# Entering the experts tile by tile beside the last products of the layer before

## The reference

```python
def rmsnorm(x, g):
    return x * rsqrt(mean(x * x, -1) + 1e-6) * g

for layer in range(2):
    h = h + mixer(rmsnorm(h, norm_mix_g[layer]))      # ends with a product by w_o
    t = rmsnorm(h, norm_ffn_g[layer])
    grp_logits = t @ w_grp + b_grp                    # 4 groups
    exp_logits = t @ w_exp + b_exp                    # 16 experts
    # best group, its two best experts, softmax weights
    for e in range(16):
        h = h + gate[:, e] * ((silu(t @ w_gate[e]) * (t @ w_up[e])) @ w_down[e])
```

## Time and profile before

| | us |
|---|---|
| median of 3 runs | 1503.54 |
| lowest, highest | 1500.58, 1504.72 |
| the profiled execution | 1504.47 |
| its span | 1502.7 |
| TensorE busy | 1370.2 |
| VectorE busy | 1030.9 |
| ScalarE busy | 854.3 |
| GpSimd busy | 390.1 |

### The profile page before, as it was taken

The page is one execution under the profiler, slowest core; times in us unless marked ns, Lnnn a source line. Parts: engine busy times, 40 slices in busy tenths (PEclk is TensorE's granted clock), DMA queues, the critical chain, the costliest instruction groups (busy, mean ns, idle before and its releaser), DMA issues. The chain is left out here.

```text
span 1502.7 us, 28124 instructions
## 1 busy us (share of the span) xinstructions
PE 1370.2 (91%) x10835; PEld 1071.2 (71%) x10835; DVE 1030.9 (69%) x1374; ACT 854.3 (57%) x1282; POOL 390.1 (26%) x431
## 2 busy tenths in 40 slices
PE   5999897988899889999998699999989899999994
PEld 3476686776774578888876587778777688888872
DVE  5366653556643599999887535775454799998996
ACT  6635551455541368888885425445552488888882
POOL 1022063446550112232323200001120122333312
PEclk9999896989989999999999899999978899999997
DMA  5222300141560689999996341221101899999984
GB/s 176 84 85 84 140 1 15 41 137 58 156 213 0 224 306 390 386 384 382 381 384 230 113 129 57 76 65 57 57 29 62 294 365 386 390 381 377 383 324 174
DMA packets 160579, 299.67 MB, mean 199 GB/s; under 512 B 16974, under 2 KB 32462, under 8 KB 160481
## 3 DMA queue, kind: packets, MB, share of 16 engines
q1 hardware_dynamic: 147968, 269.43, 50.0%
q0 software_dynamic: 11232, 24.61, 4.6%
q10 hardware_dynamic: 1280, 4.26, 0.7%
HBM read 279.96 MB, written 34.60 MB: 209 GB/s over the span
## 5 line engine op out<-in xcount | busy, mean ns | idle before, releaser
L1475 DVE TENSOR_TENSOR moe_wlo<-moe_raw,moe_whi 128x2048 fp32r<-128x2048 f32 x162 | 370.2, 2288 | 43.0 <-ACT moe_whi L1471 38.5
L1471 ACT ACTIVATE moe_whi<-moe_raw 128x2048 fp32r<-128x2048 f32 x192 | 365.3, 1918 | 43.7 <-DMA moe_raw<-in_moe_w_down_dram 19.2
L1482 PE MATMUL all_bank<-moe_whi,moe_xhi 128*128 128x512 f32 x512 | 205.2, 401 | 4.1 <-DVE moe_xlo L1531 4.1
L1483 PE MATMUL all_bank<-moe_wlo,moe_xhi 128*128 128x512 f32 x512 | 200.5, 392 | 0.0
L1484 PE MATMUL all_bank<-moe_whi,moe_xlo 128*128 128x512 f32 x512 | 200.4, 391 | 0.0
L1482 PEld LDWEIGHTS all_bank<-moe_whi,moe_xhi 128*128 128x128 f32 x512 | 96.8, 189 | 26.4 <-DVE moe_xlo L1531 4.4
L1484 PEld LDWEIGHTS all_bank<-moe_whi,moe_xlo 128*128 128x128 f32 x512 | 96.8, 189 | 21.0
L1483 PEld LDWEIGHTS all_bank<-moe_wlo,moe_xhi 128*128 128x128 f32 x512 | 97.1, 190 | 19.0
L1482 PE MATMUL all_bank<-moe_whi,moe_hhi 128*128 128x512 f32 x256 | 100.5, 392 | 4.1 <-issue 2.6
L1484 PE MATMUL all_bank<-moe_whi,moe_hlo 128*128 128x512 f32 x256 | 99.7, 389 | 0.0
L1483 PE MATMUL all_bank<-moe_wlo,moe_hhi 128*128 128x512 f32 x256 | 99.6, 389 | 0.0
(11 more groups left out here) (441 smaller groups left out, 2989.6 us busy)
## 6 DMA issues: line engine op xcount, KB each, us to landing
moe_raw<-in_moe_w_gate_dram SPq DMA_DIRECT2D x64, 1024.0 KB, 12.1
moe_raw<-in_moe_w_up_dram SPq DMA_DIRECT2D x64, 1024.0 KB, 12.5
moe_raw<-in_moe_w_down_dram SPq DMA_DIRECT2D x64, 1024.0 KB, 11.5
attn_xhat<-in_w_kv_dram SPq DMA_DIRECT2D x10, 1024.0 KB, 5.1
out_dram<-all_gain SPq DMA_DIRECT2D x16, 512.0 KB, 5.1
attn_xhat<-in_attn_w_q_dram SPq DMA_DIRECT2D x6, 1024.0 KB, 4.9
all_h<-in_rwkv_w_k_dram SPq DMA_DIRECT2D x4, 1024.0 KB, 9.5
all_h<-in_rwkv_w_v_dram SPq DMA_DIRECT2D x4, 1024.0 KB, 5.0
```

The lines of the kernel that those rows point to most:

```text
L1471: nc.scalar.activation(whi[slot % SPLITS][:, :], raw[slot % 6][:, :], ACT.Copy).then_inc(m["hi_ok"], 1)
L1475: nc.vector.tensor_tensor(wlo[slot % SPLITS][:, :], raw[slot % 6][:, :], whi[slot % SPLITS][:, :].bitcast(fp32), ALU.subtract).then_inc(m[ ...
L1482: nc.tensor.matmul(bank[b][:, :], hi[:, k0 + k, :], wh[:, k, :], start=begin and k == 0, stop=False)
L1483: nc.tensor.matmul(bank[b][:, :], hi[:, k0 + k, :], wl[:, k, :], start=False, stop=False)
```

## The change

Seven things, all in the diff:

1. A set of `front_*` functions does the experts' entry for one tile: squares by half tile with two sums, a shift (mean of the first half's squares plus epsilon) as the bias of the root, reciprocal, norm in two halves, transposes into two banks, copies (first four slices on ScalarE, last four on VectorE), logits of the tile, copy of the rows, sum of the quarters.
2. In `rwkv_chunks` and in `attention` these are placed among the last products, residuals and squares. The whole entry up to the sum of the quarters moves ahead of the meeting of engines, and `moe` starts with the first routing step. TensorE's four leading `keep_busy` matmuls are gone.
3. The normed tokens are stored by SP, one DMA for each tile of 512 KB, instead of one by ScalarE's queue.
4. SP asks for the first four weight pieces (`first_weights`) in the block before: in layer 0 when the last state copy is done, in layer 1 when the last scores are.
5. All 16 blocks of zero rows are written behind the chunks, after the load of `x`, from a part of `raw` that GpSimd clears there; the memset of `gain` in chunk 0 is gone.
6. The router's gain and weights are loaded together in chunk 2.
7. `raw`, the normed tokens and their transposes get one fixed place in SBUF for the whole program (`KEPT`), and the other tiles of each block are arranged around it.

```diff
+FRONT_BANKS = ((4, 5), (6, 7), (4, 5), (0, 1))
+
+
+def front_square(nc, g, f, j, x, junk):
+
+    nc.scalar.activation(junk, g["h"][:, j, 512 * x:512 * x + 512], ACT.Square, accum_out=f[f"part{x}"][:, j:j + 1]).then_inc(f[f"sq{x}"], 1)
+
+
+def front_shift(nc, dve, f, j):
+
+    dve.wait_ge(f["sq0"], j + 1)
+    nc.vector.tensor_scalar(f["shift"][:, j:j + 1], f["part0"][:, j:j + 1], 1.0 / D, NORM_EPS, ALU.mult, ALU.add).then_inc(f["bias"], 1)
+
+
+def front_root(nc, act, f, j):
+
+    act.wait_ge(f["sq1"], j + 1)
+    act.wait_ge(f["bias"], j + 1)
+    nc.scalar.activation(f["rms"][:, j:j + 1], f["part1"][:, j:j + 1], ACT.Sqrt, scale=1.0 / D, bias=f["shift"][:, j:j + 1]).then_inc(f["root"], 1)
+
+
+def front_tile(nc, dve, g, f, layer, j):
+
+    dve.wait_ge(f["root"], j + 1)
+    nc.vector.reciprocal(f["scale"][:, j:j + 1], f["rms"][:, j:j + 1]).then_inc(f["rstd"], 1)
+    if j == 0:
+        dve.wait_ge(g["moe_in"], 80 * (layer + 1))
+    dve.wait_ge(f["rstd"], j + 1)
+    for x in range(2):
+        at = slice(512 * x, 512 * x + 512)
+        nc.vector.scalar_tensor_tensor(out=g["xn"][:, j, at], in0=g["h"][:, j, at], scalar=f["scale"][:, j:j + 1], in1=g["gain"][:, at],
+                                       op0=ALU.mult, op1=ALU.mult).then_inc(f["xn"], 1)
+
+
+def front_store(sp, g, f, io, layer, j):
+
+    sp.wait_ge(f["xn"], 2 * j + 2)
+    sp.dma_start(io[f"xn_dram{layer}"][P * j:P * j + P, :], g["xn"][:, j, :]).then_inc(g["xn_st"], 16)
+
+
+def front_turn(nc, pe, g, f, j):
+
+    if j == 2:
+        pe.wait_ge(f["ev_a"], 1)
+        pe.wait_ge(f["ev_d"], 1)
+    for kt in range(KT):
+        if kt % 4 == 0:
+            pe.wait_ge(f["xn"], 2 * j + kt // 4 + 1)
+        ins = nc.tensor.transpose(g["bank"][FRONT_BANKS[j][kt // 4]][:, P * (kt % 4):P * (kt % 4) + P], g["xn"][:, j, P * kt:P * kt + P], g["ident"][:, :])
+        if kt % 4 == 3:
+            ins.then_inc(f["tr"], 1)
+
+
+def front_pieces(g, j, x):
+
+    return g["xnT"][:, 4 * x:4 * x + 4, P * j:P * j + P], g["bank"][FRONT_BANKS[j][x]][:, :].rearrange("p (k t) -> p k t", k=4)
+
+
+def front_copy_a(nc, act, g, f, j):
+
+    act.wait_ge(f["tr"], 2 * j + 1)
+    dst, src = front_pieces(g, j, 0)
+    nc.scalar.activation(dst, src, ACT.Copy).then_inc(f["ev_a"], 1)
+
+
+def front_copy_d(nc, dve, g, f, j):
+
+    dve.wait_ge(f["tr"], 2 * j + 2)
+    dst, src = front_pieces(g, j, 1)
+    nc.vector.tensor_copy(dst, src).then_inc(f["ev_d"], 1)
+
+
+def front_logits(nc, pe, g, f, layer, j):
+
+    if j == 0:
+        pe.wait_ge(g["moe_in"], 80 * (layer + 1))
+    for kt in range(KT):
+        if kt % 4 == 0:
+            pe.wait_ge(f["ev_d" if kt else "ev_a"], j + 1)
+        c = 32 * (kt % 4)
+        ins = nc.tensor.matmul(g["bank"][2 if j < 3 else 6][c:c + 32, P * j:P * j + P], g["wr"][:, kt, :], g["xnT"][:, kt, P * j:P * j + P], start=kt < 4, stop=kt >= 4)
+    ins.then_inc(f["lg"], 1)
+
+
+def front_rows_a(nc, act, g, f):
+
+    act.wait_ge(f["lg"], 3)
+    nc.scalar.activation(f["rows"][:, 0:3 * P], g["bank"][2][:, 0:3 * P], ACT.Copy).then_inc(f["row_a"], 1)
+
+
+def front_rows_d(nc, dve, g, f):
+
+    dve.wait_ge(f["lg"], 4)
+    nc.vector.tensor_copy(f["rows"][:, 3 * P:4 * P], g["bank"][6][:, 3 * P:4 * P]).then_inc(f["row_d"], 1)
+
+
+def front_sum(nc, pe, g, f):
+
+    for j in range(J):
+        if j == 0:
+            pe.wait_ge(f["row_a"], 1)
+        elif j == 3:
+            pe.wait_ge(f["row_d"], 1)
+        nc.tensor.matmul(g["bank"][3][:, 20 * j:20 * j + 20], f["rows"][:, P * j:P * j + P], g["quarters"][:, :], start=True, stop=True)
+
+
+def first_weights(sp, g, io, layer, pieces):
+
+    for n in pieces:
+        w = io["moe_w_gate" if n < 2 else "moe_w_up"][layer, 0, 512 * (n % 2):512 * (n % 2) + 512, :]
+        sp.dma_start(g["raw"][n][:, :].rearrange("p (k n) -> p k n", k=4), w.rearrange("(k p) n -> p k n", p=P)).then_inc(g["raw_in"][n], 16)
```

```diff
-                    sp.wait_ge(late_ok, 5)
-                    router_weights(sp, g, io, 0)
-                if 2 <= c < 10:
-                    blank_rows(2 * c - 4)
-                    blank_rows(2 * c - 3)
+                    sp.wait_ge(late_ok, 4)
+                    router_load(sp, g, io, 0)
...
             wait(sp, "rec_done", NC - 2, 2)
             inc(sp.dma_start(g["h"][:, :, :], io["x"][0].rearrange("(j p) d -> p j d", p=P)), "x_in")
-            wait(sp, "x_in", 1, 0)
+            sp.wait_ge(blank_ok, 1)
+            for e in range(16):
+                blank_rows(e)
+            wait(sp, "s_ok", NC - 1, 4)
+            first_weights(sp, g, io, 0, range(4))
+            for j in range(J):
+                front_store(sp, g, f, io, 0, j)
             sp.wait_ge(blank_st, 16 * 16)
-            router_gain(sp, g, io, 0)
-            sp.wait_ge(g["moe_in"], 80)
...
+            wait(pool, "rec_done", NC - 1, 2)
+            nc.gpsimd.memset(blank, 0.0).then_inc(blank_ok, 1)
...
+            def squares(j):
+                for x in range(2):
+                    wait(act, "h_ok", j, x + 1)
+                    if j:
+                        act.wait_ge(f[f"sq{x}"], j)
+                    front_square(nc, g, f, j, x, first_flat[:, 4 * x:4 * x + 4, :])
+
             turned_z(2)
             square_of(3)
             root(3)
+            for j in range(2):
+                squares(j)
+                front_root(nc, act, f, j)
             turned_z(3)
-            for j in range(J):
-                wait(act, "h_ok", j, 2)
-                if j:
-                    wait(act, "squared", j, 0)
-                inc(nc.scalar.activation(first_flat, g["h"][:, j, :].rearrange("p (q c) -> p q c", q=KT), ACT.Square, accum_out=g["ss"][:, j:j + 1]), "squared")
+            front_copy_a(nc, act, g, f, 0)
+            front_copy_a(nc, act, g, f, 1)
+            squares(2)
+            front_root(nc, act, f, 2)
+            front_copy_a(nc, act, g, f, 2)
+            squares(3)
+            front_root(nc, act, f, 3)
+            front_rows_a(nc, act, g, f)
+            front_copy_a(nc, act, g, f, 3)
...
+            def tile_front(j):
+                front_shift(nc, dve, f, j)
+                wait(dve, "h_ok", j, 2)
+                front_tile(nc, dve, g, f, 0, j)
...
             wait(dve, "x_in", 0, 16)
-            residual(0)
+            residual(0, 0)
+            residual(0, 1)
             variance(3)
             scale(3)
             gain(3)
             extra(3)
-            residual(1)
+            tile_front(0)
+            residual(1, 0)
+            residual(1, 1)
+            tile_front(1)
             turned_z(3)
-            residual(2)
-            residual(3)
+            front_copy_d(nc, dve, g, f, 0)
+            residual(2, 0)
+            residual(2, 1)
+            front_copy_d(nc, dve, g, f, 1)
+            tile_front(2)
+            residual(3, 0)
+            front_copy_d(nc, dve, g, f, 2)
+            front_shift(nc, dve, f, 3)
+            residual(3, 1)
+            wait(dve, "h_ok", 3, 2)
+            front_tile(nc, dve, g, f, 0, 3)
+            front_copy_d(nc, dve, g, f, 3)
+            front_rows_d(nc, dve, g, f)
...
             product(1)
             product(2, range(0, 8))
             turn(3)
+            front_turn(nc, pe, g, f, 0)
             product(2, range(8, 16))
-            product(3)
+            wait(pe, "zt_a", 3, 1)
+            wait(pe, "zt_d", 3, 1)
+            front_turn(nc, pe, g, f, 1)
+            product(3, range(0, 8))
+            front_turn(nc, pe, g, f, 2)
+            product(3, range(8, 16))
+            wait(pe, "h_ok", 3, 1)
+            for j in range(3):
+                front_logits(nc, pe, g, f, 0, j)
+            front_turn(nc, pe, g, f, 3)
+            front_logits(nc, pe, g, f, 0, 3)
+            wait(pe, "h_ok", 3, 2)
+            front_sum(nc, pe, g, f)
```

```diff
-                first = isinstance(e, int) and e == 0
-                todo = [("gate", 0, e), ("gate", 1, e)] + ([] if first else [("down", 0, e - 1), ("down", 1, e - 1)]) + [("up", 0, e), ("up", 1, e)]
+                if isinstance(e, int) and e == 0:
+                    return
+                todo = [("gate", 0, e), ("gate", 1, e), ("down", 0, e - 1), ("down", 1, e - 1), ("up", 0, e), ("up", 1, e)]
...
-            act.wait_ge(xn_ok, J)
-            act.dma_start(xn_dram.rearrange("(j p) d -> p j d", p=P), xn[:, :, :]).then_inc(xn_st, 16)
-            for kt in range(0, KT, 2):
-                act.wait_ge(tr, kt + 1)
-                nc.scalar.activation(xnT[:, kt, :], bank[kt][:, :], ACT.Copy).then_inc(ev_a, 1)
...
-            dve.wait_ge(lgT_done, 1)
-            V.tensor_copy(lgT[:, :], bank[0][:, :]).then_inc(lgT_ok, 1)
-            dve.wait_ge(lg_done, 1)
-            tt(lg[:, :, :], bank[1][:, 0:J * (NG + NE)].rearrange("p (j n) -> p j n", j=J),
+            tt(lg[:, :, :], bank[3][:, 0:J * (NG + NE)].rearrange("p (j n) -> p j n", j=J),
                br[:, :].rearrange("p (x n) -> p x n", x=1).to_broadcast([P, J, NG + NE]), ALU.add)
...
             keep_busy(12)
```

(47 more changed lines are left out.)

119 lines of the change are left out of this document (56 added, 63 removed).

## The result

On the first chip the kernel after took 1486.08 us (median, 1480.61 to 1492.17) against 1504.13 for before: ratio 0.9889, interval 0.9847 to 0.9931. Timed again three times, on other chips, it was 0.9929 (0.9904 to 0.9954), 0.9912 (0.9889 to 0.9936) and 0.9920 (0.9894 to 0.9945), that is 10.1 to 12.2 us faster. So about 11 us are gained where 5.3 were forecast. The 18 us between the first two medians come from four executions of each, which spread over 9 to 12 us; no later timing repeats them, and I take the excess of some 7 us as chance.

The account below looks back on a forecast made before the run. Loops run at their own pace; the entry chains before routing, about 30 us with hardly a product, set their start. 4.0 - 0.7 + 4.0 - 2.0 = 5.3 us gained: 1498.2 against 1503.54, range 1493 to 1503.

Parts of the forecast that it names:

- What the change can move: Expert loops of both layers: they run at their own pace, so only the moment each begins can move.
- Zero rows behind the chunks: 0.: Chunk loop: moving the zero stores gains nothing, since none of the loop's waits named a DMA.
- The spread: Whole kernel: its own runs lie 4.1 us apart, so a change under 0.3% (4.5 us) can't be told from none.
- Entry of layer 0: Last product to first routing step, layer 0: routing at 507.9 instead of 511.88, 4.0 us gained, less 0.7 for the clock.
- Entry of layer 1: Last product to first routing step, layer 1: routing at 1165.3, 4.0 us gained at full clock, less 2.0 for the clock.
- First weights early: 0.: Expert block's entry: asking early for four weight pieces gains 0, as no wait for these pieces existed.
- The clock behind the entry: Behind each entry: keep-busy matmuls take 5.84 us at half clock, not 2.92, making the rank matmul 0.5 late.
- rival B: Entries and behind the routing: clock falls less than today, 8 + 2.6, so 10.6 us gained, 1493; chance 0.17.
- A: Whole kernel, the forecast itself: 4.5 to 7.5 us gained, 1496 to 1499; chance 0.42.
- D: Both entries: clock at half from the last product's end on, 4.6 us slower in all, 1508; chance 0.09.

Follow-up runs that it names:

- align: Kernel before with 32 bytes of padding ahead of the attention's split activations, starting them at byte 190720 instead of 190688: 1497.72 us against 1502.31, ratio 0.9965.
- z_behind: Kernel before with only the sixteen zero-row stores moved out of the chunk loop, behind the load of the residual stream: 1498.94 us against 1501.30, ratio 0.9984.
- z_back2: Kernel after with the zero rows put back in the chunks, two per chunk, and the gain loaded behind them: 1490.00 us beside after_again's 1490.81.
- after_again: Kernel after, unchanged, profiled and timed again on another chip: 1490.81 us.
- order2: Kernel after with quarter sums of tiles 0 to 2, tile 2's turn and VectorE's copies placed earlier at the entries: 1485.57, 1485.16 and 1486.84 us.
- w_late: Kernel after with each layer's first four weight pieces asked for at the expert block's start again: 1496.25 us (0.9961) beside after_again's 1490.81.
- align_z: Kernel before with both the 32 bytes of attention padding and the zero rows moved behind the chunks: 1494.49 us against 1502.85, ratio 0.9944.
- h_align: order2 with 32 bytes of padding ahead of the constants and h, and again ahead of the gain: 1489.70 us, ratio 0.9906 to before.

## Why the prediction was wrong

The direction was right and the size too small: 5.3 us forecast, 18 by the first median, 10 to 12 in the three later timings.

*What the change can move.* "So a loop runs at its own pace ... What the change can move is the moment at which each loop begins." This step failed. The change also moves tensors in memory, and the sum has no term for that. align measured 4.6 us for it. All 960 matmuls with 512 columns in the attention read one of the four moved tensors (the expectation of align counted 672); 0.006 us each make up to 6 us, where TensorE is what the stage waits for. The row was there: 2.8 us for 12 matmuls is 0.233 each, and the loops of the same kernel run at 0.227. I used the 2.8 as a price and did not ask why it wasn't 2.7.

*Zero rows behind the chunks: 0.* Mis-sized by 0 to 3 us (z_behind 2.4, z_back2 beside after_again nothing), and the reason was wrong. "None of the chunk loop's waits named a DMA" is true, but late instruction loads have no name in the waits; they stand under "issue". The test that I had set, "if the chunks change their length", can't be read from one profile, since it swings by 10 us.

*The spread.* "This kernel's own runs lie 4.1 us apart" was read from three executions. Before spread over 13 us on one chip (1496.21 to 1509.16 in 23), so neither the range nor the first median was as firm as it looked.

*Entry of layer 0.* 4.0 - 0.7 = 3.3 forecast; the table gives 78.8 to 75.6 or 74.5, so 3.2 to 4.3. The products became 2.6 us longer by the turns (3.6 forecast), the tail from the last product's end took 9.0 or 7.9 where 7.2 were forecast. The forecast counted one quarter sum behind the last copy where the kernel has all four (1.07 us at full clock, 1.90 at half). That the term comes out is partly luck: two errors nearly cancel.

*Entry of layer 1.* 4.0 - 2.0 = 2.0 forecast. With equal pace, align's 27.6 to 25.6 or 26.9: 0.7 to 2.0; misaligned, 29.0 to 26.9: 2.1. The size was near, its terms not: the clock cost nothing in two executions of after and 1.3 us in the other two, not 2.0; in its place VectorE was later and the turn of tile 3 stood behind the logits of tile 2, which order2 took away (23.7).

*First weights early: 0.* Right for the sum as far as the runs show, but the argument was from before's order (15.5 us between entry and first split). In the new order the cover is gone; w_late shows what it is worth.

*The clock behind the entry.* From the routing to layer 1's first product it is 0.9 to 1.3 us less, with 10.4 us at half clock on this way in before and 3 to 7 in after. That is the kind of term that rival B named, at half its size or less (2.6). It needs no new entry, though: align, with the old one, has 19.6 us and 3.7 at half. What decides where the clock falls is not shown.

Of the rivals, A's 4.5 to 7.5 us is near what the table shows for the entries, 3.9 to 6.3 (align_z leaves them 2 to 5). B, 10.6 gained, came near the time mostly for a wrong reason: it has no padding in it. D did not happen. Together: 4.6 for the padding, about 5 for the entries, 0 to 3 for the zero rows are 10 to 13 us, against 10.1 to 12.2 measured. Of these only the padding is measured by an edit of its own whose interval is clear of none; the entries are read from the timelines. Open stays why one execution of after has its chunks at half clock for 7 us and another for 24, and why 31 of the 95 pauses lie further behind a packet.

## What to carry to other kernels

Read where the tensors lie, before and after, when a diff changes allocations, and compare the pace of like matmuls between stages. A difference of 3% between two stages of one kernel is a fault to find and not a price. When a gain is seen in a stretch that the change doesn't touch, profile the same kernel again before explaining it. When work is moved ahead of a boundary, look at what it covered behind it.

## What the hardware showed that I had not expected

Operands of matmuls of 512 columns that start at a multiple of 32 bytes and not of 64 slow them from 0.227 to 0.233 us each, here for tensors read as either operand; the starts tried were 190688 and 92448 against 190720 and 92416. The chunks' matmuls of 64 columns didn't react to the place of h (h_align). Instruction packets of 16 KB come late among bulk transfers, and TensorE goes on 2.1 to 2.6 us behind the start of a late one: in before's chunks after a pause of 3.02 us, behind which the granted clock fell to half, from 0.96 in 316 to 320 to 0.50 in 320 to 328. Not every such pause is followed by half clock: in after 1.69 us at the same place were not. Twice the zero rows cost 9.2 us; that all of it comes this way is not shown. One sixteenth costs the same as none.
